# The up-projection of a conv FFN as one level of Strassen's block algorithm

## The reference, cut to what matters

```python
def conv_ffn(x, norm_g, w_up, conv_w, conv_b, w_down):
    u = rms_norm(x, norm_g) @ w_up                      # 2048x1024 @ 1024x5632
    u = causal_depthwise_conv(u, conv_w) + conv_b       # 3 taps
    gate, val = jnp.split(u, 2, axis=-1)
    return (jax.nn.silu(gate) * val) @ w_down
```

## Time and profile before

| | us |
|---|---|
| median of 3 runs | 3243.14 |
| lowest, highest | 3238.62, 3243.97 |
| span of the profiled execution | 3242.0 |
| TensorE busy in it | 3131.6 (97%) |
| VectorE, ScalarE, GpSimd busy | 1558.3, 820.5, 231.4 |

### The profile page before, as it was taken

One profiled execution on the slowest core, in us unless ns is written; L12 is line 12 of the kernel. 1 busy time (PEld: TensorE's weight loads), 2 busy tenths in 40 slices (PEclk: granted clock), 3 DMA queues, 4 the chain that ended last, 5 costly groups with the idle time before them and its releaser, 6 DMA issues. The chain is left out here.

```text
span 3242.0 us, 38109 instructions
## 1 busy us (share of the span) xinstructions
PE 3131.6 (97%) x15590; PEld 2454.7 (76%) x15590; DVE 1558.3 (48%) x1560; ACT 820.5 (25%) x1152; POOL 231.4 (7%) x185
## 2 busy tenths in 40 slices
PE   7999999988999988999999999999999999999999
PEld 5778887855565655887788888888887788788787
DVE  6334553136557544543845544554455533432743
ACT  5221212123433533211411111111111422321421
POOL 0000000013344341000000000000000000000000
PEclk9999999989999999999999999999999999999999
DMA  3442222257576454443311011111101634424542
GB/s 138 151 137 72 70 66 77 63 156 204 133 208 182 133 143 153 162 133 116 118 52 44 33 52 52 52 52 52 51 26 65 227 128 165 169 101 148 166 141 68
DMA packets 230321, 361.45 MB, mean 111 GB/s; under 512 B 39645, under 2 KB 124125, under 8 KB 221885
## 3 DMA queue, kind: packets, MB, share of 16 engines
q1 hardware_dynamic: 226398, 339.62, 33.5%
q0 software_dynamic: 3808, 20.22, 1.7%
HBM read 262.37 MB, written 96.94 MB: 111 GB/s over the span
## 5 line engine op out<-in xcount | busy, mean ns | idle before, releaser
L90 PE MATMUL up_ps<-up_h_hi,up_w_hi 128*128 128x512 f32 x1408 | 549.4, 390 | 2.1 <-DVE up_h_lo L1838 1.5
L92 PE MATMUL up_ps<-up_h_hi,up_w_lo 128*128 128x512 f32 x1408 | 547.8, 389 | 0.0
L91 PE MATMUL up_ps<-up_h_lo,up_w_hi 128*128 128x512 f32 x1408 | 547.8, 389 | 0.0
L90 PE MATMUL inp_ps<-inp_h_hi,carry_q 128*128 128x512 f32 x896 | 353.2, 394 | 12.4 <-DVE inp_h_lo L189 9.6
L91 PE MATMUL inp_ps<-inp_h_lo,carry_q 128*128 128x512 f32 x896 | 349.9, 390 | 0.0
L92 PE MATMUL inp_ps<-inp_h_hi,carry_k_two 128*128 128x512 f32 x896 | 349.8, 390 | 0.0
L90 PEld LDWEIGHTS up_ps<-up_h_hi,up_w_hi 128*128 128x128 f32 x1408 | 264.3, 188 | 59.5 <-issue 4.4
L91 PEld LDWEIGHTS up_ps<-up_h_lo,up_w_hi 128*128 128x128 f32 x1408 | 264.4, 188 | 55.4 <-issue 0.7
L92 PEld LDWEIGHTS up_ps<-up_h_hi,up_w_lo 128*128 128x128 f32 x1408 | 264.3, 188 | 54.8
L1990 DVE TENSOR_TENSOR carry_squares<-up_ps,carry_rows 128x2048 f32<-128x2048 f32 x42 | 96.3, 2292 | 417.3 <-PE up_ps L92 416.9
L90 PE MATMUL down_banks<-down_a_hi,down_w_hi 128*128 128x512 f32 x704 | 277.0, 393 | 15.5 <-DVE down_a_lo L2216 8.9
(11 more groups left out here) (322 smaller groups left out, 4554.7 us busy)
## 6 DMA issues: line engine op xcount, KB each, us to landing
carry_room<-in_w_up_dram SPq DMA_DIRECT2D x42, 512.0 KB, 5.7
act<-carry_room SPq DMA_DIRECT2D x21, 1024.0 KB, 4.6
carry_room<-act SPq DMA_DIRECT2D x7, 2816.0 KB, 13.3
down_a_second<-act SPq DMA_DIRECT2D x7, 2816.0 KB, 18.2
carry_room<-cum_rows SPq DMA_DIRECT2D x16, 1024.0 KB, 6.8
carry_room<-x SPq DMA_DIRECT2D x8, 2048.0 KB, 9.3
carry_room<-in_w_in_dram SPq DMA_DIRECT2D x26, 512.0 KB, 5.8
xbc<-carry_room SPq DMA_DIRECT2D x12, 1024.0 KB, 5.7
```

Of the source, the lines that this page charges most:

```text
L90: pe.matmul(out, w_hi, x_hi, start=first, stop=False)
L91: pe.matmul(out, w_hi, x_lo, start=False, stop=False)
L92: return pe.matmul(out, w_lo, x_hi, start=False, stop=last)
```

## The change

The weights of a pair of tiles and the tokens are seen as 2x2 blocks: two halves of the 1024 input features by gate and value tile, and two halves of the features by two blocks of 512 tokens. Such a group (one pair, 1024 tokens) is 8 products of 512 features x 512 tokens; Strassen's method (in Winograd's form) computes the same 4 output blocks from 7 products of sums and differences, A11, S1, S2, A12, S3, A22, S4 by the name of their weight operand. A product is 4 x 3 = 12 matmuls. There are 2 rounds (halves of the tokens) of 22 pairs, so 44 groups, g = 0 to 43, and 308 products, in the order of `UpOrder`.

- Tokens are normalised, by gain and `rstd`, before they are split. `x_hi` and `x_lo` hold the seven token operands. GpSimd and VectorE form those of the first round when the phase begins. Those of the second round are prepared by GpSimd in four pieces (`ahead`, at g = 12, 14, 16, 18) from x1 loaded for it (`load_near`), stored to DRAM (`store_ahead`, seven DMAs each) and loaded when the first round has done with a place (`load_ahead`).
- GpSimd forms the weight operands S1 to S4 of each group, four operations of 128x512. ScalarE makes the high part of one operand per product, VectorE the low part, in a ring of 7 places: at step s they make the operand of step s + 7.
- Some products are accumulated onto others in PSUM; ScalarE copies intermediate sums to SBUF (`take`), VectorE adds them at the eviction (`evict`), 512 columns at a time. The convolution runs over 1024 tokens; the last two columns of each tile are kept for the second round (`halo`).
- Out-projection: `rstd` of the first two blocks is computed there; its TensorE and ScalarE loops are written out. Down-projection: the clearing of `sums` is moved, and the last store is awaited later.

```diff
@@ out_projection @@
+            def add_up(n):
+                pe.wait_ge(added, (n + 2) * KD + KD)
+                pe.wait_ge(halved, 3 * n + 6)
+                pe.matmul(banks[:, KD - 1], carry.ones[:, :], sums[:, n], start=True, stop=True).then_inc(summed, 1)
...
@@ up_projection @@
+class UpOrder:
...
+    NEED = (0, 3, 1, 2, 4, 5, 6)
+    RING = 7
...
+        for r in range(self.ROUNDS):
+            first = r * self.PAIRS
+            for v in self.NEED:
+                self.steps += [(first, v), (first + 1, v)]
+            for g in range(first + 2, first + self.PAIRS):
+                self.steps.append((g, 0))
+                if g > first + 2:
+                    self.steps.append((g - 1, 6))
+                self.steps += [(g, v) for v in (1, 2, 3, 4, 5)]
+            self.steps.append((first + self.PAIRS - 1, 6))
...
+        def bank(g, v):
+            return banks[:, 4 * (g % 2) + {A11: 0, S2: 0, S3: 0, S1: 1, S4: 1, A12: 2, A22: 3}[v]]
...
+            def s1(g):
+                wait_raw(pool, g)
+                if g > 0:
+                    pool.wait_ge(wlo, done(g - 1, S1))
+                    pool.wait_ge(s2_s, g)
+                r = raw(g)
+                pool.tensor_tensor(s_one[:, :], r[:, 0:512], r[:, 512:1024], ALU.add).then_inc(s1_s, 1)
+            def s2(g):
+                pool.wait_ge(s1_s, g + 1)
+                if g > 0:
+                    pool.wait_ge(wlo, done(g - 1, S2))
+                    pool.wait_ge(s4_s, g)
+                pool.tensor_tensor(s_two[:, :], s_one[:, :], raw(g)[:, 1024:1536], ALU.subtract).then_inc(s2_s, 1)
+            def s3(g):
+                r = raw(g)
+                pool.wait_ge(s1_s, g + 1)
+                pool.tensor_tensor(r[:, 0:512], r[:, 1024:1536], r[:, 0:512], ALU.subtract).then_inc(s3_s, 1)
+            def s4(g):
+                pool.wait_ge(s2_s, g + 1)
+                pool.wait_ge(wlo, done(g, A12))
+                r = raw(g)
+                pool.tensor_tensor(r[:, 1536:2048], r[:, 1536:2048], s_two[:, :], ALU.subtract).then_inc(s4_s, 1)
...
+            def ahead(q):
+                pool.wait_ge(near_in, 32 * (q + 1))
+                pool.wait_ge(inverted, 2)
+                if q > 0:
+                    pool.wait_ge(xv_st, 16 * 7 * q)
+                for i, (b, k) in enumerate(((2, q), (2, Q + q), (3, q), (3, Q + q))):
+                    pool.tensor_scalar(near[:, i], near[:, i], g_col[:, k:k + 1], None, ALU.mult).then_inc(scaled, 1)
+                    pool.wait_ge(scaled, Q + 4 * q + i + 1)
+                    pool.tensor_tensor(near[:, i], near[:, i], rstd[b], ALU.mult).then_inc(near_n, 1)
+                pool.wait_ge(near_n, 4 * q + 4)
+                pool.tensor_tensor(far[:, 0], near[:, 2], near[:, 0], ALU.subtract).then_inc(far_s, 1)
+                pool.tensor_tensor(far[:, 1], near[:, 3], near[:, 2], ALU.subtract).then_inc(far_s, 1)
+                pool.wait_ge(far_s, 4 * q + 2)
+                pool.tensor_tensor(far[:, 2], far[:, 1], near[:, 0], ALU.add).then_inc(far_s, 1)
+                pool.wait_ge(far_s, 4 * q + 3)
+                pool.tensor_tensor(far[:, 3], near[:, 1], far[:, 2], ALU.subtract).then_inc(far_s, 1)
...
+            for g in range(2, G):
+                s1(g)
+                s2(g)
+                s3(g)
+                s4(g)
+                if g == 5:
+                    add_squares()
+                if g in BACK:
+                    ahead(BACK.index(g))
...
+            def load_raw(g):
+                into = raw(g)
...
+                elif g > 3:
+                    sp.wait_ge(wlo, max(done(g - 2, S4), done(g - 2, A22)))
+                for b in range(2):
+                    t = 2 * (g % PAIRS) + b
+                    sp.dma_start(into[:, b * 1024:(b + 1) * 1024], w_tiles[t * P:(t + 1) * P, :]
+                                 ).then_inc(raw1_in if g == 1 else w_in_s[g % 2], 16)
+            def store(g):
+                r, j = divmod(g, PAIRS)
+                sp.wait_ge(out_s, g + 1)
+                sp.dma_start(act_t[j * P:(j + 1) * P, r * HALF:(r + 1) * HALF], conv[1]
+                             ).then_inc(carry.act_stored if g == G - 1 else stored, 16)
+            def store_ahead(q):
+                sp.wait_ge(far_s, 4 * q + 4)
+                for v, at in ((A11, near[:, 0]), (A12, near[:, 1]), (S4, near[:, 3]), (S1, far[:, 0]), (S3, far[:, 1]),
+                              (S2, far[:, 2]), (A22, far[:, 3])):
+                    sp.dma_start(xv[v][:, q, :], at).then_inc(xv_st, 16)
...
+            for g in range(2, G):
+                if g % PAIRS == 2:
+                    store(g - 2)
+                if g + 2 < G:
+                    load_raw(g + 2)
+                if g % PAIRS != 2 and g != PAIRS:
+                    store(g - 2)
+                if g == 11:
+                    sp.wait_ge(summed, 2)
+                    load_near(0)
+                if g - 2 in BACK:
+                    q = BACK.index(g - 2)
+                    store_ahead(q)
+                    if q + 1 < Q:
+                        load_near(q + 1)
...
+            def weights(s):
+                g, v = steps[s]
+                if s >= RING:
+                    act.wait_ge(mm, s - RING + 1)
+                if v in (A11, A12, A22):
+                    wait_raw(act, g)
+                else:
+                    act.wait_ge({S1: s1_s, S2: s2_s, S3: s3_s, S4: s4_s}[v], g + 1)
+                act.activation(w_hi[:, s % RING], source(g, v), ACT.Copy).then_inc(whi, 1)
...
+            def take(g, v):
+                act.wait_ge(mm, done(g, v))
+                if v == A11:
+                    if g == 0:
+                        act.wait_ge(carry.x1_stored, 16)
+                    else:
+                        act.wait_ge(c11_s, g)
+                    act.activation(p1c, bank(g, v), ACT.Copy).then_inc(p1c_s, 1)
+                elif v == S2:
+                    if g > 1:
+                        act.wait_ge(c12_s, g - 1)
+                    act.activation(u2c[g % 2], bank(g, v), ACT.Copy).then_inc(u2c_s, 1)
+                else:
+                    if g > 0:
+                        act.wait_ge(c21_s, g)
+                        act.wait_ge(c22_s, g)
+                    act.activation(u3c, bank(g, v), ACT.Copy).then_inc(u3c_s, 1)
...
+                if v == A11 and j != 1 or v == S2 or v == S3 and j != 1:
+                    take(g, v)
+                if v == A12 and j == 1:
+                    take(g, A11)
+                if v == A22 and j == 1:
+                    take(g, S3)
+                weights(s + RING)
+                if v == A22 and j == 1 or v == A11 and j > 2:
+                    silu(g - 1)
+                if v == S4 and j in (1, PAIRS - 1):
+                    silu(g)
...
+            def evict(g, v):
+                b, at, copy, ready, evicted = {
+                    A12: (1, 0, p1c, p1c_s, c11_s), S4: (1, 1, u2c[g % 2], u2c_s, c12_s),
+                    A22: (0, 0, u3c, u3c_s, c21_s), S1: (0, 1, u3c, u3c_s, c22_s)}[v]
+                dve.wait_ge(mm, done(g, v))
+                dve.wait_ge(ready, g + 1)
...
+                dve.tensor_tensor(pre[b][:, 2 + at * 512:2 + (at + 1) * 512], bank(g, v), copy, ALU.add).then_inc(evicted, 1)
...
+            def convolve(g, b):
+                r, j = divmod(g, PAIRS)
+                for s in (c11_s, c12_s) if b else (c22_s, c21_s):
+                    dve.wait_ge(s, g + 1)
+                if r > 0:
+                    dve.tensor_copy(pre[b][:, 0:2], halo[:, j, b]).then_inc(halo_s, 1)
+                    dve.wait_ge(halo_s, 2 * g + b + 1)
+                if b == 0 and g > 0:
+                    dve.wait_ge(out_s, g)
+                if b == 1 and g > 0:
+                    dve.wait_ge(stored, 16 * g)
+                dve.tensor_scalar(conv[b], pre[b][:, 2:2 + HALF], conv_w[:, j, b, 2:3], None, ALU.mult).then_inc(tap, 1)
+                done_taps[0] += 1
+                for c in range(2):
+                    dve.wait_ge(tap, done_taps[0])
+                    out = dve.scalar_tensor_tensor(out=conv[b], in0=pre[b][:, c:c + HALF], scalar=conv_w[:, j, b, c:c + 1], in1=conv[b],
+                                                   op0=ALU.mult, op1=ALU.add)
+                    if c == 0:
+                        out.then_inc(tap, 1)
+                        done_taps[0] += 1
+                    else:
+                        out.then_inc(convd, 1)
+                if r == 0:
+                    dve.tensor_copy(halo[:, j, b], pre[b][:, HALF:HALF + 2]).then_inc(halo_s, 1)
+            def finish(g):
+                dve.wait_ge(convd, 2 * g + 2)
+                dve.wait_ge(gated, g + 1)
+                dve.scalar_tensor_tensor(out=conv[1], in0=conv[1], scalar=conv_b[:, g % PAIRS, 1:2], in1=conv[0], op0=ALU.add, op1=ALU.mult
+                                         ).then_inc(out_s, 1)
...
+                if v == A12 and j != 1:
+                    evict(g, A12)
```

(61 more changed lines are left out.)

548 lines of the change are left out of this document (290 added, 258 removed).

## The result

| | before | after |
|---|---|---|
| median (lowest to highest) of 3 runs, us | 3243.14 (3238.62 to 3243.97) | 3519.72 (3519.6 to 3525.03) |
| span of the profiled execution | 3242.0 | 3517.7 |
| ScalarE's entry into the stage to the last multiply's end | 968.9 | 1252.7 |

The ratio is 1.0861 (95% interval 1.0842 to 1.0881): slower by 8.6%. The forecast was 3542, 22 us or 0.6% more.

What follows compares the result with a forecast made beforehand. VectorE, at 26.4 us per group against TensorE's 19.05, was taken to become the bound. Stage terms summed to 1268.7 us against 968.9 (+299.8), giving 3542 us with small effects elsewhere; range 3320 to 3650.

Steps and rivals of the forecast that it cites:

- boundary of the halves: Up-projection, between the two token rounds: VectorE's queue takes 80.2 us, including three GpSimd bursts and a 3.2 us wait.
- Which engine is the bound: Up-projection: VectorE's cycle with its waits, 26.4 us per group, exceeds TensorE's 19.05, so TensorE idles 7 us per group.
- Group of 26.4 us: Steady up-projection group on VectorE: 15.65 own work, 0.5 for ScalarE, 6.0 for the store, 4.2 for GpSimd.
- store wait: VectorE's convolution waits for a store queued behind two weight loads on SyncE: 6.0 us per group, bounds 3.1 and 7.5.
- VectorE's own work: Per group: seven low parts, four evictions, two convolutions, last multiply and two small copies, 15.65 us without the added waits.
- GpSimd beside VectorE: VectorE and GpSimd wait for each other's instructions; four GpSimd sums cost VectorE 4.2 us per group, bounds 0 and 5.2.
- rival A: Up-projection: wide VectorE operations don't wait for GpSimd; cycle 22.2 us, total 3349 us; chance 0.17.
- Three late loads: At g = 14, 16, 18 GpSimd waits for a late x1 load, delaying VectorE's weight: 21 us each, 63 in all.
- Squares, reciprocals, first preparation: Up-projection extras: two reciprocals of 3.35 us, GpSimd's sum of squares and first token preparation beside VectorE, 14.7 us together.
- Last groups: Groups 42 and 43 load no weights, so they have no wait for the store: 2 x 20.4 = 40.8 us.
- Around the stage: Outside the up-projection: out-projection +1.5 us, down-projection -2.1 us from the moved memset, awaited last store 0.
- Rival C: Up-projection: VectorE keeps ahead and TensorE stays the bound from group 3; 3152 us, or 3215 with late loads; chance 0.06.

Runs made afterwards that it cites:

- experiment 1: Changed kernel with SyncE's store of group g-2 issued ahead of the weight loads of g+2 in every round: 3302.6 us, ratio 1.0194.
- 3: Changed kernel with the store ahead of the weight loads and the token stores and x1 loads one SyncE round earlier: 3256.1 us, ratio 1.0055.
- version 5: Changed kernel with the store first, GpSimd's token operations moved between S3 and S4, and x1 therefore loaded earlier: 3221.4 us, ratio 0.9939.
- 7: version 5 with GpSimd making only 8 of 512 columns of each weight combination from group 2 on: 3186.3 us, ratio 0.9841.
- 8: version 5 with the two-column halo copies made by ScalarE in place of VectorE: 3219.7 us, ratio 0.9940.
- experiment 4: Changed kernel with GpSimd making only 8 of 512 columns of each weight combination from group 2 on: 3408.3 us, ratio 1.0519.
- experiment 9: Changed kernel with GpSimd making S1 and S2 of each group twice, same result: 3604.7 us, ratio 1.1129.
- Experiment 2: Changed kernel with the token combination stores and the next x1 load issued one SyncE round earlier: 3465.8 us, ratio 1.0693.
- experiment 6: Changed kernel with the store of g-2 issued between the two weight loads of g+2: 3473.1 us, ratio 1.0723.

## Why the prediction was right, step by step

| stretch of the stage, us | forecast | measured |
|---|---|---|
| ScalarE's entry to the end of group 2's first convolution | 114 | 110.3 |
| 19 groups to g = 21, with squares, first preparation, late loads | 579.3 | 580.3 |
| boundary of the halves, 3 groups | 80.2 | 80.2 |
| 17 groups to g = 41 | 448.8 | 443.1 |
| groups 42 and 43 | 40.8 | 33.2 |
| last eviction, convolution, multiply | 5.6 | 5.6 |
| sum | 1268.7 | 1252.7 |

(All rows go from the end of one group's first convolution to that of another's, as in the forecast. In the second row errors cancel: the ordinary groups of the first half are 0.7 us shorter than forecast, 13 in all, the late loads 10 longer and the squares and reciprocals 4.5. The terms of the boundary were not measured one by one; that they sum to the same number may be chance.)

- **Which engine is the bound.** Right. TensorE was busy 935 of 1252 us (75%, 70 forecast), at 0.87 of its clock; experiments 1, 3, 5, 7 and 8 make it the bound again at 18.98 to 19.04 us a group, against the 7 x 2.72 = 19.05 of the earlier trace rows.
- **Group of 26.4 us.** 26.07. By its terms: the store wait 7.25 us for 6.0, GpSimd's part 3.4 for 4.2 (experiment 4), ScalarE's 0.54 for 0.5, VectorE's own work 26.07 - 7.2 - 0.54 - 3.4 = 14.9 for 15.65 (low parts and evictions follow each other after 0.60 us, as at 2410.89 and 2411.49, not 0.62 and 0.67, and the last multiply takes 1.3 with its wait, not 1.45). The store wait was 1.25 us too short, GpSimd's part 0.8 and VectorE's own work 0.75 too long; that they cancelled is luck.
- **The store wait, 36 times.** The mechanism was right and proved by the order alone (experiment 1). The size was off by 1.2: from the first load's issue to the store's landing the sum had 0.46 + 5.3, from the pair of loads of the earlier trace rows, and it is 0.85, the issue of both loads, and 6.2. The bound of 7.5, with the 5.7 that the loop's loads have in the median, was nearer.
- **GpSimd beside VectorE.** Right for operations of 128 partitions, which no row of before had shown, so rival A was wrong. 4, 9 and the rows agree: 3.4 us for four instructions. Where they fall was partly wrong: in the steady groups of the second half none on the wide taps (1285 ns with full and 1284 with small sums; in experiment 9 they do wait there, 1740), and 1.1 us on the copies of two columns, which the forecast had not counted. By the rule of the Trainium skill (SBUF — State Buffer, "SBUF: two separate sides") a wait falls on VectorE operations with two SBUF inputs or in a 2-port mode: low parts and wide taps fit, and evictions with one input in PSUM don't wait, as measured. The first tap and the copy of two columns have one SBUF tensor as input and wait as well (1.74 for 0.75, 1.25 for 0.16); whether these run in such a mode no run here shows.
- **Three late loads.** Groups 14, 16 and 18 last 51.9 to 52.7 us, 26 to 27 over 25.7, and groups 13, 15 and 17 are 2.2 shorter: 73 us in all, 24 for each load where I had 21. Counted from the low part of S4 at 2022.0, the load was there after 18.3 us (2040.3), 14.7 by my count, and GpSimd's twelve operations took 16.8 us, not 13.6. GpSimd's own idle time, 25.8 us, was forecast as 16: it begins 7.5 us before that low part. Experiment 2 removes 54 of the 73.
- **Squares, reciprocals, first preparation.** 14.7 forecast; groups 4, 5, 8, 11 and 12 are together 19 over 25.7 each.
- **Last groups.** 7.6 us too many. Low parts are made seven products ahead, so six of the fourteen fall before these groups, and of GpSimd's bursts, which the 20.4 us held for each group, one instruction falls into them (at 2758.4); I had taken out neither. Group 43 still waits 4.8 us for TensorE and ScalarE.
- **Around the stage.** The part before the stage was not 1.5 us later but 5.5 earlier (ScalarE enters at 1534.69 instead of 1540.16). In the nine experiments, whose code before that point is the same, the first low part starts from 1532.1 to 1539.3: this is scatter between executions. After it 730.3 us for 732.9: -2.6, -2.1 forecast, where the experiments scatter from 728.0 to 730.9. Of the 23.5 us by which the span stayed below 3541.2, 16 are in the stage, 7 before it.
- **Rival C**, the change doing what it is for, was off by one thing it named itself: "6.0 us of DMA inside its loop". Version 5 is short of C's 3152 by some 70 us, in the start, the boundary, groups 4 and 8, which hold the reciprocals, and groups 10 to 17.

## What to carry to other kernels

Saving one product in eight of a stage by cleverness pays only if the engine next in line has time: here TensorE's group fell from 21.8 to 19.05 us, and VectorE needed 18.4 to 19.0 with everything in order and 26 with one store misplaced. In each in-order queue, look for work that is ready behind work that is not: a store of finished data behind loads that wait cost 217 us, and was repaired by exchanging two lines. And place optional work where its engine idles anyway, not ahead of the operand that the next engine wants first (version 5, 35 us less, perhaps a part of it from the earlier load).

## What the runs showed of the hardware

- A store of 512 KB lands 2.7 us after its issue with nothing ahead of it (experiment 1), 5.0 behind one load of 512 KB (experiment 6), 6.2 behind two (changed kernel), in the median of 44 stores each.
- A GpSimd tensor_tensor of 128x512 beside VectorE costs VectorE 0.85 to 1.0 us (3.4 for four, 2.0 for two more); on evictions from PSUM of the same size it costs nothing (681 to 688 ns in every version). It takes 1.26 us where it waits for nothing, and mostly 1.6 to 1.8, at times 2.3, beside VectorE; GpSimd's tensor_scalar of the same size takes 1.56, not the 0.8 that I had estimated.
- A copy of 128x2 on VectorE takes 0.16 us and 1.25 when it meets GpSimd, 1.1 more; the first tap, of 1024 columns, takes 1.0 more (1.74 for 0.75). The wait is not set by the size of what waits.
